# Turned products as three of 256 columns into one half bank, multiplied by the token row straight out of the bank

## The chip, the cores and the metric

The kernel runs on one NeuronCore of one Trainium2 chip. The metric is the time of one execution on the device in microseconds (us). TensorE (PE in the profile, with its loads of weights as PEld) multiplies, VectorE (DVE) and ScalarE (ACT) work on tiles in SBUF and in the eight banks of PSUM, SyncE (SP) issues the transfers, and GpSimd (POOL) a few small ones.

## The reference

Two transformer blocks on 256 tokens of width 2048, in float32. Cut to the lines that hold the large products:

```python
def first_block(x, ...):
    h = rmsnorm(x, attn_norm[l])
    qkv = jnp.einsum('bsd,de->bse', h, w_qkv[l])
    ...                                   # three attentions: y_a, y_b, y_c
    y = jnp.concatenate([y_a, y_b, y_c], axis=-1)
    x = x + jnp.einsum('bse,ed->bsd', y, w_o[l])
    h = rmsnorm(x, ffn_norm[l])
    g = causal_dwconv(jnp.einsum('bsd,df->bsf', h, w_gate[l]), conv_w[l], conv_b[l])
    u = jnp.einsum('bsd,df->bsf', h, w_up[l])
    x = x + jnp.einsum('bsf,fd->bsd', jax.nn.silu(g) * u, w_down[l])
    return rmsnorm(x, final_norm)
```

The second block projects `rmsnorm(x)` by `w_in` and two low rank paths, attends (latent attention, top-k attention, and a cross attention to 256 memory tokens), and ends with `x + square(relu(hm @ w_up)) @ w_down` and a last norm. Hidden widths are 5632 and 8192. The norm of a token is one number for each token, so it can be applied behind a product: it is the kernel's "token row".

## The kernel before

**Split numbers.** Every float32 operand of a large product is split into a high part, which TensorE's fp32r mode takes whole, and the rest: hi and lo. A product is then hi x hi + hi x lo + lo x hi. Activations stand as `xT[P, k, h, token]` (h = 0 hi, 1 lo; `mT` and `cT` likewise), turned so that the contracted dimension lies on the 128 partitions.

**Units.** The weights, 424 MB in all, pass once through the chip in 804 units of 1024 columns (512 KB). SP's queue brings a unit into one of four slots of `raw_w`, ScalarE writes `hi_w` (L840), VectorE writes `lo_w = raw_w - hi_w` (L1270), and PE uses both. The three engines each run the same list of units; `units(n)` in each engine's program takes the next n, with the splits running three units ahead of the products. Between calls of `units` stands the work of the attentions and norms, in an order written by hand.

**Groups.** Units form groups, each of which fills two banks, and the groups alternate between banks 0, 1 and 2, 3; PE starts a group when the group two before it has left its banks (`bank_out`). There are two kinds:
- straight groups (v, o, down, tail, and others; L465 to L467): a tile of 128 tokens of the activation is loaded as the weights of the array, and 512 columns of the streamed matrix pass through it, three products for each tile of 128 of the contracted dimension. The output has tokens on its partitions.
- turned groups (qk, gate, up1, q_nope, k_nope, kx, qx, up2; 104 groups): a 128 x 128 tile of the matrix is loaded, and the 256 tokens pass. The output has features on its partitions and is `out.T`. Each of a group's two tiles of 128 features has a bank of its own. These groups have up to 16 tiles of the contracted dimension and 4 units.

**A turned product before.** `w_hi` is loaded once and hi and lo of the activation pass together as 512 columns (L456): hi x hi goes to the first half of the bank, hi x lo to the second. `w_lo` then passes the 256 columns of hi, into the first half (L458). The two halves are added when the bank is emptied: ScalarE copies the second half out (L861, `part_out`), VectorE adds the first half to it (L1284, `sum_out`), and for the stages in `ROWED` VectorE multiplies the sum by the token row (L1289, `rowed`).

**What follows in the MLPs.** For a pair of gate tiles ScalarE makes the base of the convolution (L867), VectorE adds two taps (L1293, L1296), ScalarE takes tanh (L871) and VectorE forms silu (L1301). In up1 VectorE multiplies 0.5 x silu x up (L1307) and then by the token row (L1310), ScalarE writes the high part of the result (L877) and VectorE the low part (L1276). In up2 VectorE multiplies by the token row (L1317) and squares the positive part (L1320), then the same two parts follow (L883, L1276). L501 spreads a token row over the partitions; L482 and L512 are transposes.

## Time and profile before

| | |
|---|---|
| time, median of 3 runs | 2459.22 us (2454.11 to 2463.85) |
| the profiled execution | 2454.48 us, its span 2452.7 us |
| TensorE busy | 2403.1 us, 98% of the span |
| weight loads (PEld) | 2012.3 us |
| VectorE busy | 1562.8 us, 64% |
| ScalarE busy | 1248.1 us, 51% |
| DMA | 432.13 MB, mean 176 GB/s |
| mean granted clock | 0.996 |

The page gives busy time as the union of what an engine's instructions cover. Matmuls are pipelined: a product's record is longer than the distance from its start to the next one's, so the rate of TensorE is read from starts, in the timeline. A load of weights (PEld) lies beside the product before it.

### The profile page before, as it was taken

To read this page: it belongs to the slowest core of one execution; us is meant where nothing else is said; L and a number is where in the kernel's file an instruction comes from. 1 tells how busy PE (TensorE), PEld (TensorE's weight loads), DVE (VectorE), ACT (ScalarE), POOL (GpSimd) and SP (SyncE) were. 2 spreads that over 40 slices of the span, in tenths; PEclk is the share of its full clock that TensorE was granted. 3 is DMA by queue.
4 is the path that set the end of the run, shared out by engine and by line. 5 is a ranking of instruction groups with operands and counts; after the bars stand their busy time and mean duration, and the time that the engine had idled before them with its cause. 6 is when DMAs were issued, how large, how long until landed. Compare 5 with 4: busy or idle time off the path is not lost.

```text
span 2452.7 us, 32017 instructions
## 1 busy us (share of the span) xinstructions
PE 2403.1 (98%) x12314; PEld 2012.3 (82%) x12314; DVE 1562.8 (64%) x2437; ACT 1248.1 (51%) x1954; POOL 5.2 (0%) x12
## 2 busy tenths in 40 slices
PE   7999999999999999999999999999999999999998
PEld 6888877788888888888877877887888888888886
DVE  5687777777777557755667544664766556556454
ACT  5466566555555435544556445655544344344343
POOL 0000000000000000000000000000000000000000
PEclk9999999999999999999999999999999999999999
DMA  6544444455555565566564544554565665665664
GB/s 232 168 159 155 137 155 138 155 185 193 198 181 193 195 188 180 194 210 187 165 192 144 172 131 135 185 166 132 172 196 182 197 180 196 190 188 185 212 188 138
DMA packets 119063, 432.13 MB, mean 176 GB/s; under 512 B 13264, under 2 KB 13536, under 8 KB 118400
## 3 DMA queue, kind: packets, MB, share of 16 engines
q1 hardware_dynamic: 117936, 424.70, 54.3%
q0 software_dynamic: 976, 5.39, 0.6%
q8 instruction: 98, 1.61, 0.3%
q14 instruction: 53, 0.43, 0.1%
HBM read 427.93 MB, written 2.11 MB: 175 GB/s over the span
## 4 chain that ended last, share of the span: by engine, by line
PE 92%; DVE 4%; ACT 2%; issue 1%; DMA 1%; SPq 0%; ACTq 0%; DVEq 0%
PE bank L456 28%; PE bank L465 15%; PE bank L467 15%; PE bank L466 15%; PE bank L458 14%; DVE lo_w L1270 1%; PE bank L653 1%; DVE xT L1409 1%; ACT hi_w L840 1%; PE bank L482 1%; ACT xT L944 0%; DMA raw_w<-in_w_qk 0%; PE bank L637 0%; PE bank L526 0%; PE bank L607 0%
## 5 line engine op out<-in xcount | busy, mean ns | idle before, releaser
L1270 DVE TENSOR_TENSOR lo_w<-raw_w,hi_w 128x1024 fp32r<-128x1024 f32 x804 | 965.9, 1218 | 631.0 <-ACT hi_w L840 630.0
L840 ACT ACTIVATE hi_w<-raw_w 128x1024 fp32r<-128x1024 f32 x804 | 833.8, 1052 | 606.3 <-PE bank L467 417.8
L456 PE MATMUL bank<-xT,hi_w 128*128 128x512 f32 x3008 | 1054.0, 395 | 0.0
L458 PE MATMUL bank<-xT,lo_w 128*128 128x256 f32 x3008 | 839.5, 279 | 0.0
L456 PEld LDWEIGHTS bank<-xT,hi_w 128*128 128x128 f32 x3008 | 565.8, 188 | 128.8 <-issue 0.3
L458 PEld LDWEIGHTS bank<-xT,lo_w 128*128 128x128 f32 x3008 | 568.8, 189 | 0.5
L465 PE MATMUL bank<-hi_w,act_hi 128*128 128x512 f32 x864 | 341.4, 395 | 0.0
L467 PE MATMUL bank<-hi_w,act_lo 128*128 128x512 f32 x864 | 341.2, 395 | 0.0
L466 PE MATMUL bank<-lo_w,act_hi 128*128 128x512 f32 x864 | 341.2, 395 | 0.0
L465 PE MATMUL bank<-hi_w,xT 128*128 128x512 f32 (+1 forms) x736 | 294.2, 400 | 4.3 <-DVE xT L1409 3.5
L467 PE MATMUL bank<-hi_w,xT 128*128 128x512 f32 (+1 forms) x736 | 286.7, 389 | 0.0
L466 PE MATMUL bank<-lo_w,xT 128*128 128x512 f32 (+1 forms) x736 | 286.0, 389 | 0.0
L465 PEld LDWEIGHTS bank<-hi_w,act_hi 128*128 128x128 f32 x864 | 162.1, 188 | 39.5
L467 PEld LDWEIGHTS bank<-hi_w,act_lo 128*128 128x128 f32 x864 | 162.1, 188 | 39.5
L466 PEld LDWEIGHTS bank<-lo_w,act_hi 128*128 128x128 f32 x864 | 162.1, 188 | 38.9
L465 PEld LDWEIGHTS bank<-hi_w,xT 128*128 128x128 f32 x736 | 138.8, 189 | 32.0 <-issue 4.8
L467 PEld LDWEIGHTS bank<-hi_w,xT 128*128 128x128 f32 x736 | 138.6, 188 | 28.9
L466 PEld LDWEIGHTS bank<-lo_w,xT 128*128 128x128 f32 x736 | 138.9, 189 | 25.3
L1276 DVE TENSOR_TENSOR act_lo<-steps,act_hi 128x512 fp32r<-128x512 f32 x54 | 37.4, 693 | 39.3 <-ACT act_hi L883 23.6
L867 ACT ACTIVATE steps<-product,gains 128x256 f32<-128x256 f32 x44 | 26.5, 602 | 66.3 <-DVE product L1289 66.3
L861 ACT ACTIVATE product<-bank 128x256 f32<-128x256 f32 x88 | 33.4, 380 | 37.6 <-PE bank L458 37.6
L883 ACT ACTIVATE act_hi<-steps 128x512 fp32r<-128x512 f32 x32 | 20.3, 633 | 63.5 <-DVE steps L1320 63.5
(315 smaller groups left out, 1586.5 us busy)
## 6 DMA issues: line engine op xcount, KB each, us to landing
raw_w<-in_w_up SPq DMA_DIRECT2D x216, 512.0 KB, 4.2
raw_w<-in_w_down SPq DMA_DIRECT2D x216, 512.0 KB, 3.6
raw_w<-in_w_gate SPq DMA_DIRECT2D x88, 512.0 KB, 3.7
raw_w<-in_w_in SPq DMA_DIRECT2D x72, 512.0 KB, 3.8
raw_w<-in_w_qk SPq DMA_DIRECT2D x64, 512.0 KB, 3.6
raw_w<-in_w_v SPq DMA_DIRECT2D x32, 512.0 KB, 4.0
raw_w<-in_w_o SPq DMA_DIRECT2D x32, 512.0 KB, 3.5
raw_w<-in_w_out SPq DMA_DIRECT2D x32, 512.0 KB, 3.6
```

Source lines behind the costliest of these rows:

```text
L456: e.matmul(pair[c][:, :], w_hi[:, cols_k], both[:, kt].rearrange("p h t -> p (h t)"), start=(kt == 0), stop=False, skip_group_check=True)
L458: last = e.matmul(pair[c][:, 0:TOK], w_lo[:, cols_k], both[:, kt, 0, :], start=False, stop=(kt == g.kts - 1), skip_group_check=True)
L465: e.matmul(out, in_hi[:, at, rows], w_hi[:, cols_k], start=(kt == 0), stop=False)
L466: e.matmul(out, in_hi[:, at, rows], w_lo[:, cols_k], start=False, stop=False)
L467: last = e.matmul(out, in_lo[:, at, rows], w_hi[:, cols_k], start=False, stop=(kt == g.kts - 1))
L482: last = e.transpose(bank[:, k * TOK + t * P:k * TOK + (t + 1) * P], src[:, t, kt * P:(kt + 1) * P], const("ident"))
L653: last = e.matmul(banks[7][:, 0:wide], pT[:, k * P:(k + 1) * P], head_values(family, h, k), start=(k == 0), stop=(k == kts - 1))
L840: e.activation(hi_w[:, u % SPLIT_SLOTS, 0:unit_cols[u]], raw_w[:, u % RAW_SLOTS, 0:unit_cols[u]], ACT.Copy).then_inc(s["w_hi"], 1)
L861: e.activation(out, group_banks(n)[c][:, TOK:2 * TOK], ACT.Copy, scale=scale).then_inc(s["part_out"], 1)
L867: e.activation(conv1[:, pair % 2, c], out, ACT.Identity, bias=gain("convb", tile), scale=gain("conv2", tile)).then_inc(s["conv_base"], 1)
L1270: e.tensor_tensor(lo, raw_w[:, u % RAW_SLOTS, 0:unit_cols[u]], hi.bitcast(F32), ALU.subtract).then_inc(s["w_lo"], 1)
L1276: e.tensor_tensor(lo, prod[:, pair % 2], hi.bitcast(F32), ALU.subtract).then_inc(s[f"act_lo{tag}_done"], 1)
```

## The change

The two products for a tile of the contracted dimension become three, all of 256 columns and all into the first half of the bank: hi weights with hi, the same hi weights with lo, lo weights with hi. The second half of the bank is no longer used, so ScalarE's copy goes. VectorE empties the bank alone: with a scale, or with a scale and the token row in one instruction, straight out of the bank (`up2` is now among the stages in `ROWED`). In `up1` it multiplies 0.5 x silu by the bank directly; the token row of that stage is multiplied into silu in the gate group instead. Waits on `part_out` and `rowed` become waits on `w_used` and `sum_out`.

```diff
-ROWED = {"qk": "attn", "gate": "ffn", "kx": "mem", "qx": "cross"}
+ROWED = {"qk": "attn", "gate": "ffn", "kx": "mem", "qx": "cross", "up2": "mlp"}
...
                                 both = turned_in(g.stage)
                                 cols_k = slice(k * TURNED_COLS + c * P, k * TURNED_COLS + (c + 1) * P)
-                                e.matmul(pair[c][:, :], w_hi[:, cols_k], both[:, kt].rearrange("p h t -> p (h t)"),
-                                         start=(kt == 0), stop=False, skip_group_check=True)
-                                last = e.matmul(pair[c][:, 0:TOK], w_lo[:, cols_k], both[:, kt, 0, :],
-                                                start=False, stop=(kt == g.kts - 1), skip_group_check=True)
+                                out = pair[c][:, 0:TOK]
+                                e.matmul(out, w_hi[:, cols_k], both[:, kt, 0, :], start=(kt == 0), stop=False)
+                                e.matmul(out, w_hi[:, cols_k], both[:, kt, 1, :], start=False, stop=False)
+                                last = e.matmul(out, w_lo[:, cols_k], both[:, kt, 0, :],
+                                                start=False, stop=(kt == g.kts - 1))
...
             def diff_scores(i):
                 h, t = i // 2, i % 2
                 W, _ = token_tile(t)
-                e.wait_ge(s["rowed"], max(row_count["qk", h], row_count["qk", 8 + h]))
+                e.wait_ge(s["sum_out"], max(sum_count["qk", h], sum_count["qk", 8 + h]))
                 if i:
...
             def turned_group(g, n):
-                for c in range(2):
-                    tile, pair = 2 * g.part + c, g.part
-                    out, scale = turned_out(g.stage, tile)
-                    e.wait_ge(s["w_used"], 2 * g.last + 1 + c)
-                    if g.stage == "gate" and pair:
-                        e.wait_ge(s["prod1"], pair)
-                    if g.stage == "up1":
-                        e.wait_ge(s["conv_taps"], 4 * pair + 2 * (c + 1))
-                    if g.stage == "up2" and pair >= 2:
-                        e.wait_ge(s["act_lo2_done"], pair - 1)
-                    e.activation(out, group_banks(n)[c][:, TOK:2 * TOK], ACT.Copy,
-                                 scale=scale).then_inc(s["part_out"], 1)
-                    if g.stage == "gate":
-                        e.wait_ge(s["rowed"], row_count["gate", tile])
+                pair = g.part
+                if g.stage == "gate":
+                    for c in range(2):
+                        tile = 2 * pair + c
+                        e.wait_ge(s["sum_out"], sum_count["gate", tile])
                         if pair >= 2:
                             e.wait_ge(s["act_lo1_done"], pair - 1)
-                        e.activation(conv1[:, pair % 2, c], out, ACT.Identity, bias=gain("convb", tile),
+                        e.activation(conv1[:, pair % 2, c], product1[:, c, :], ACT.Identity, bias=gain("convb", tile),
                                      scale=gain("conv2", tile)).then_inc(s["conv_base"], 1)
-                if g.stage == "gate":
                     e.wait_ge(s["conv_taps"], 4 * pair + 4)
+                    if pair >= 2:
+                        e.wait_ge(s["act_lo1_done"], pair - 1)
                     e.activation(prod1[:, pair % 2], conv1[:, pair % 2], ACT.Tanh,
                                  scale=0.5).then_inc(s["gate_tanh"], 1)
                 elif g.stage == "up1":
                     if pair >= PHASE:
                         e.wait_ge(s["w_used"], 2 * (last_unit[f"down1_{pair // 8 - 2}"] + 1))
-                    e.wait_ge(s["prod1"], pair + 1)
+                    e.wait_ge(s["sum_out"], sum_count["up1", 2 * pair + 1])
                     e.activation(act_slot(pair, act_hi1, act_lo1)[0], prod1[:, pair % 2],
                                  ACT.Copy).then_inc(s["act_hi1_done"], 1)
...
             def turned_group(g, n):
+                pair, row = g.part, ROWED.get(g.stage)
+                if row:
+                    e.wait_ge(s["row_copied"], ROW[row] + 1)
+                if g.stage == "up1":
+                    pr = prod1[:, pair % 2]
+                    e.wait_ge(s["gate_rowed"], pair + 1)
                 for c in range(2):
-                    tile, pair = 2 * g.part + c, g.part
+                    tile, bank = 2 * pair + c, group_banks(n)[c][:, 0:TOK]
+                    e.wait_ge(s["w_used"], 2 * g.last + 1 + c)
+                    if g.stage == "up1":
+                        e.scalar_tensor_tensor(pr[:, c], pr[:, c], 0.5, bank, ALU.mult,
+                                               ALU.mult).then_inc(s["sum_out"], 1)
+                        continue
                     out, scale = turned_out(g.stage, tile)
-                    e.wait_ge(s["part_out"], sum_count[g.stage, tile])
-                    e.scalar_tensor_tensor(out, group_banks(n)[c][:, 0:TOK], scale, out,
-                                           ALU.mult, ALU.add).then_inc(s["sum_out"], 1)
-                    if g.stage in ROWED:
-                        e.wait_ge(s["sum_out"], sum_count[g.stage, tile])
-                        e.wait_ge(s["row_copied"], ROW[ROWED[g.stage]] + 1)
-                        e.tensor_tensor(out, out, token_rows[ROWED[g.stage]][:, :], ALU.mult).then_inc(s["rowed"], 1)
+                    if g.stage == "gate" and pair:
+                        e.wait_ge(s["conv_base"], 2 * pair)
+                        e.wait_ge(s["conv_taps"], 4 * pair)
+                    if g.stage == "up2" and pair >= 2:
+                        e.wait_ge(s["prod2"], pair - 1)
+                    if row:
+                        e.scalar_tensor_tensor(out, bank, scale, token_rows[row][:, :],
+                                               ALU.mult, ALU.mult).then_inc(s["sum_out"], 1)
+                    else:
+                        e.tensor_scalar(out, bank, scale, None, ALU.mult).then_inc(s["sum_out"], 1)
                     if g.stage == "gate":
                         after = conv1[:, pair % 2, c]
+                        e.wait_ge(s["sum_out"], sum_count["gate", tile])
                         e.wait_ge(s["conv_base"], 2 * pair + c + 1)
                         e.scalar_tensor_tensor(after[:, 1:TOK], out[:, 0:TOK - 1], gain("conv1", tile),
                                                after[:, 1:TOK], ALU.mult, ALU.add).then_inc(s["conv_taps"], 1)
...
                     e.wait_ge(s["gate_tanh"], pair + 1)
                     e.scalar_tensor_tensor(pr, pr, 1.0, conv1[:, pair % 2], ALU.add,
                                            ALU.mult).then_inc(s["gate_silu"], 1)
+                    e.wait_ge(s["gate_silu"], pair + 1)
+                    e.tensor_tensor(pr, pr, row_ffn[:, :].unsqueeze(1).to_broadcast([P, 2, TOK]),
+                                    ALU.mult).then_inc(s["gate_rowed"], 1)
                 elif g.stage == "up1":
-                    pr = prod1[:, pair % 2]
-                    e.wait_ge(s["gate_silu"], pair + 1)
                     e.wait_ge(s["sum_out"], sum_count["up1", 2 * pair + 1])
-                    e.scalar_tensor_tensor(pr, pr, 0.5, product1[:, :, :], ALU.mult,
-                                           ALU.mult).then_inc(s["prod_half"], 1)
-                    e.wait_ge(s["prod_half"], pair + 1)
-                    e.tensor_tensor(pr, pr, row_ffn[:, :].unsqueeze(1).to_broadcast([P, 2, TOK]),
-                                    ALU.mult).then_inc(s["prod1"], 1)
                     act_low(pair, 1, act_hi1, act_lo1, prod1)
                 elif g.stage == "up2":
                     cv = conv2[:, pair % 2]
                     e.wait_ge(s["sum_out"], sum_count["up2", 2 * pair + 1])
-                    e.wait_ge(s["row_copied"], ROW["mlp"] + 1)
-                    e.tensor_tensor(cv, cv, row_mlp[:, :].unsqueeze(1).to_broadcast([P, 2, TOK]),
-                                    ALU.mult).then_inc(s["up2_rowed"], 1)
-                    e.wait_ge(s["up2_rowed"], pair + 1)
+                    if pair >= 2:
+                        e.wait_ge(s["act_lo2_done"], pair - 1)
                     e.scalar_tensor_tensor(prod2[:, pair % 2], cv, 0.0, cv, ALU.max, ALU.mult).then_inc(s["prod2"], 1)
                     act_low(pair, 2, act_hi2, act_lo2, prod2)
```

On PE, at the start of the program, the first unit of qk (bank0 is the first tile's bank; L482 are the transposes ahead of it) stood before as:

```order
L482 MATMUL bank7<-consts,x 128x128 x4
L456 MATMUL bank0<-xT,hi_w 128x512
L458 MATMUL bank0<-xT,lo_w 128x256
L456 MATMUL bank0<-xT,hi_w 128x512
L458 MATMUL bank0<-xT,lo_w 128x256
```

and stands now as:

```order
L480 MATMUL bank7<-consts,x 128x128 x4
L454 MATMUL bank0<-xT,hi_w 128x256
L455 MATMUL bank0<-xT,hi_w 128x256
L456 MATMUL bank0<-xT,lo_w 128x256
L454 MATMUL bank0<-xT,hi_w 128x256
```

Two rows for a tile have become three, of 768 columns in all as before; each row stands for a load of weights and a product, so there is one load more too.

On VectorE, in the first MLP, one gate group (bank0, bank1) and the up1 group behind it (bank2, bank3), with the four splits of weights between them, stood before as:

```order
L1284 SCALAR_TENSOR_TENSOR product1<-bank0,product1 128x256
L1289 TENSOR_TENSOR product1<-product1,row1 128x256
L1293 SCALAR_TENSOR_TENSOR steps1<-product1,gains,steps1 128x255
L1296 SCALAR_TENSOR_TENSOR steps1<-product1,gains,steps1 128x254
...
L1301 SCALAR_TENSOR_TENSOR steps1<-steps1 128x512
L1270 TENSOR_TENSOR lo_w<-raw_w,hi_w 128x1024 x4
L1284 SCALAR_TENSOR_TENSOR product1<-bank2,product1 128x256
L1284 SCALAR_TENSOR_TENSOR product1<-bank3,product1 128x256
L1307 SCALAR_TENSOR_TENSOR steps1<-steps1,product1 128x512
L1310 TENSOR_TENSOR steps1<-steps1,row1 128x512
L1276 TENSOR_TENSOR act_lo1<-steps1,act_hi1 128x512
```

and stands now as:

```order
L1290 SCALAR_TENSOR_TENSOR product1<-bank0,row1 128x256
L1298 SCALAR_TENSOR_TENSOR steps1<-product1,gains,steps1 128x255
L1301 SCALAR_TENSOR_TENSOR steps1<-product1,gains,steps1 128x254
...
L1306 SCALAR_TENSOR_TENSOR steps1<-steps1 128x512
L1309 TENSOR_TENSOR steps1<-steps1,row1 128x512
L1260 TENSOR_TENSOR lo_w<-raw_w,hi_w 128x1024 x4
L1280 SCALAR_TENSOR_TENSOR steps1<-steps1,bank2 128x256
L1280 SCALAR_TENSOR_TENSOR steps1<-steps1,bank3 128x256
L1266 TENSOR_TENSOR act_lo1<-steps1,act_hi1 128x512
```

The row product behind each gate bank has gone into the instruction that empties it, and the 512 column row product has moved from behind the up1 banks to ahead of the four splits.

## Rows read from the trace of the kernel before

**Rows 1.** The page: span, busy shares, clock by slice, chain.
```profile
span 2452.7 us, 32017 instructions
...
PE 2403.1 (98%) x12314; PEld 2012.3 (82%) x12314; DVE 1562.8 (64%) x2437; ACT 1248.1 (51%) x1954; POOL 5.2 (0%) x12
...
PEclk9999999999999999999999999999999999999999
...
PE 92%; DVE 4%; ACT 2%; issue 1%; DMA 1%; SPq 0%; ACTq 0%; DVEq 0%
```

**Rows 2.** PE's groups by form: engine, operation, shapes, count | busy, mean ns.
```profile
L456 PE MATMUL bank<-xT,hi_w 128*128 128x512 f32 x3008 | 1054.0, 395 | 0.0
L458 PE MATMUL bank<-xT,lo_w 128*128 128x256 f32 x3008 | 839.5, 279 | 0.0
...
L456 PE MATMUL bank<-mT,hi_w 128*128 128x512 f32 x64 | 24.4, 419 | 0.0
...
L456 PE MATMUL bank<-cT,hi_w 128*128 128x512 f32 x48 | 17.8, 408 | 0.5 <-DVE q_nT L1284 0.5
```

**Rows 3.** PE's timeline, up2 stage, 70 pairs: start, length (us), instruction.
```profile
1799.88 0.39 PE L456 MATMUL bank<-xT,hi_w 128*128 128x512 f32 x1
1800.11 0.28 PE L458 MATMUL bank<-xT,lo_w 128*128 128x256 f32 x1
1800.23 0.39 PE L456 MATMUL bank<-xT,hi_w 128*128 128x512 f32 x1
...
1823.80 0.39 PE L456 MATMUL bank<-xT,hi_w 128*128 128x512 f32 x1
```

**Rows 4.** PE's timeline, a straight stage on xT, first and last of 32.
```profile
1242.75 0.39 PE L465 MATMUL bank<-hi_w,xT 128*128 128x512 f32 x1
...
1249.78 0.39 PE L466 MATMUL bank<-lo_w,xT 128*128 128x512 f32 x1
```

**Rows 5.** PE's timeline, last down stage, first and last of 66.
```profile
2299.77 0.40 PE L465 MATMUL bank<-hi_w,act_hi 128*128 128x512 f32 x1
...
2314.94 0.39 PE L467 MATMUL bank<-hi_w,act_lo 128*128 128x512 f32 x1
```

**Rows 6.** PE's timeline, tail stage, first and last of 40.
```profile
1206.78 0.34 PE L465 MATMUL bank<-hi_w,xT 128*128 128x400 f32 x1
...
1213.90 0.34 PE L465 MATMUL bank<-hi_w,xT 128*128 128x400 f32 x1
```

**Rows 7.** PE's timeline, kx stage, behind a wait of PE.
```profile
1623.56 0.63 PE L456 MATMUL bank<-mT,hi_w 128*128 128x512 f32 x1
1623.99 0.41 PE L458 MATMUL bank<-mT,lo_w 128*128 128x256 f32 x1
1624.20 0.63 PE L456 MATMUL bank<-mT,hi_w 128*128 128x512 f32 x1
```

**Rows 8.** Busy time by stretch, with the granted clock (PEclk).
```profile
core 0: us, PE busy (x) PEld busy (x) DVE busy (x) ACT busy (x) POOL busy (x), PEclk, DMA share, GB/s
1623.20:1625.20 2.00, 2.00 (x7) 1.69 (x7) 1.56 (x2) 0.00 (x0) 0.00 (x0) 0.50 0.73 244
```

**Rows 9.** PE's timeline, sixteen transposes on end and what follows.
```profile
1383.54 1.91 PE L512 MATMUL bank<-consts,staging 128*128 128x128 f32 x16
1385.20 0.48 PE L465 MATMUL bank<-hi_w,xT 128*128 128x512 f32 x1
```

**Rows 10.** ScalarE's groups by form, one of them.
```profile
L861 ACT ACTIVATE product<-bank 128x256 f32<-128x256 f32 x88 | 33.4, 380 | 37.6 <-PE bank L458 37.6
```

**Rows 11.** VectorE's groups by form.
```profile
L1317 DVE TENSOR_TENSOR steps<-steps,row 128x512 f32<-128x512 f32 x32 | 22.2, 693 | 1.1
...
L1289 DVE TENSOR_TENSOR product<-product,row 128x256 f32<-128x256 f32 x44 | 18.7, 425 | 1.5
L1307 DVE SCALAR_TENSOR_TENSOR steps<-steps,product 128x512 f32<-128x512 f32 x22 | 15.2, 693 | 2.7 <-DVE product L1284 0.5
L1310 DVE TENSOR_TENSOR steps<-steps,row 128x512 f32<-128x512 f32 x22 | 15.2, 692 | 0.7
```

**Rows 12.** PE's waits: line, for whom, total us, times, longest.
```profile
PE bank L501 <- DVE row_attn L1396: 4.6, 1, 4.6
PE bank L501 <- DVE row L1396: 4.4, 2, 2.3
...
PE bank L653 <- ACT a_pT L1043: 2.6, 6, 0.5
...
PE bank L775 <- ACT q_idxT L959: 0.8, 1, 0.8
...
PE bank L456 <- DVE q_nT L1284: 0.5, 1, 0.5
```

21 lines of the change are left out of this document (9 added, 12 removed).

## The prediction

> **What bounds the kernel now.** I read the page first: its busy shares, its row of the clock and its chain of work. TensorE is busy for 2403.1 of 2452.7 us, its granted clock is at the upper level (2.4 GHz) in every slice, and 92% of the chain that ended last is PE [rows 1]. VectorE and ScalarE have slack everywhere in the long stages. So a change that lightens them can give back at most the time in which PE stands still, 2452.7 - 2403.1 = 49.6 us, and a change to the products themselves counts in full.
>
> The second view groups PE's instructions by form. The turned stages make 3008 + 64 + 48 = 3120 pairs of a 512 column and a 256 column product [rows 2]; their durations there (395 and 279 ns) overlap, so they don't add up. What a product costs is the time from its start to the start of the next, and that stands in the timeline.
>
> Third, the timeline in four stretches without a wait. In the up2 stage the 512 column product starts at 1799.88 and the 69th after it at 1823.80 [rows 3]: 23.92 / 69 = 0.3467 us for a pair of 768 columns. In a straight stage that reads xT, 31 steps of 512 columns take 1249.78 - 1242.75 = 7.03 us, 226.8 ns each [rows 4]. In a down stage 65 such steps take 15.17 us, 233.4 ns each [rows 5]. In the tail stage 39 steps of 400 columns take 7.12 us, 182.6 ns each [rows 6].
>
> Last, the same pair while the granted clock is 0.50, its lower level (1.2 GHz), just after PE had waited: 1624.20 - 1623.56 = 0.64 us, that is 768 columns at exactly one per clock [rows 7, 8]. So columns alone would take 768 / 2.4 = 320.0 ns at the upper level, and each step there has something on top: 26.7 ns in a turned pair, 13.5 ns in the 512 column step on xT (213.3 for the columns), 20.1 ns in the down step, 15.9 ns in the 400 column step (166.7). This surplus is the number on which the case turns.
>
> **The change, part by part.**
> *Products.* For each of the 3120 pairs PE now runs three products of 256 columns, each with its own load of 128 x 128 weights. The columns are the same 768. What is added is one more product and one more load per pair: 3120 of each. The trace has no 256 column product of this type behind another, so I bound its step. From below: in the pair, the step that starts with the 256 column product lasts 0.11 to 0.12 us (1800.11 to 1800.23), and the other 0.23 [rows 3]. If the surplus goes with the columns (26.7 / 768 = 0.035 ns a column), three steps again take 346.7 ns and the edit costs nothing; if the shortest reading, 0.11, held for all three, 330 ns, it would give 16.7 x 3120 = 52 us back. The columns (320 ns) don't exclude that, but the two readings of a pair must sum to 346.7, so 0.11 is mostly the rounding of a row. From above: each product with its load pays the surplus of a down step, 20.1 ns, so that three take 3 x (106.7 + 20.1) = 380.4 ns, 33.7 more than now, x 3120 = 105 us.
>
> Between them I take a surplus per product of 13.35 ns. Two rows speak for it. The surplus of 400 columns (15.9 ns) isn't smaller than that of 512 on the same tile (13.5 ns), so it doesn't shrink with the columns [rows 4, 6]. And 26.7 ns for the two products of a pair is just twice 13.35, beside 13.5 for a lone 512 column product, where by columns the pair should have 1.5 times 13.5 = 20.2 [rows 3, 4]. That the 256 column step reads shorter than 120 ns (106.7 + 13.35) I explain by where the start is drawn: a load that is still being read can hold up the step behind it, and the two steps share 26.7 ns. With it three products take 320 + 40 = 360.0 ns, 13.3 more than now, and 3120 x 13.3 = **41.6 us** more on the path. This falls on PE, which has no cover.
>
> Can PE's loads or the feeding of instructions become the limit instead? Sixteen 128 column products with a load each pass in 1385.20 - 1383.54 = 1.66 us, 104 ns for load and product [rows 9]. That is below 115, so neither binds at 115 to 120 ns, at least in a run of 16; a longer run isn't in the trace.
>
> *ScalarE.* It no longer copies the second half bank: 208 instructions (two tiles for each of the 104 turned groups) at about 380 ns [rows 10], 79 us. All of that lies beside PE.
>
> *VectorE.* The product with the token row is folded into the one that empties the bank. Removed are 84 row products of 256 columns at 425 ns (32 qk, 44 gate, 4 kx, 4 qx), the 22 products L1307, which become part of emptying the up1 banks, and 32 of 512 columns in up2 at 693 ns: about 36 + 15 + 22 = 73 us, also beside PE [rows 11]. One is moved: the row product of the 22 pairs (692 ns) [rows 11] now stands in the gate group, ahead of the next four splits of weights. But VectorE starts that group without ScalarE's 380 ns copy, and without the 425 ns row product behind its last bank, so the splits come 0.69 - 0.38 - 0.425 = 0.1 us earlier than now. Emptying a bank now waits for PE directly, and nothing new is queued between.
>
> *Waits of PE.* Those that a lighter VectorE or ScalarE could shorten are small: 0.5 us before the first q_nope products, 2.6 us of values waiting for a copied a_pT, 0.8 us for a copied q_idxT, and others no longer than that. The largest, 4.6 and 4.4 us before L501, are for the token rows themselves, which come from sums over x and not from a turned group [rows 12]. The rows named here sum to 3.9 us and the smaller ones behind them perhaps double that, so I bound this at 0 and 10 us of the 49.6, and take 2, the lower part, since q_nT alone is emptied by a changed instruction.
>
> The sum against the profiled execution, 2454.5 us outside its span of 2452.7: 2454.5 + 41.6 - 2 = 2494 us. This execution was 4.7 us below the median of the three runs (2459.2), whose own spread is 10 us; against the median the sum is 2499. I predict 2497 us.
>
> **The rivals.**
> *A, the forecast, 50%:* a surplus per product and load, 2485 to 2515 us.
>
> *B, the surplus goes with the columns: no difference.* The direct reading speaks for it: the 256 column step lasts 0.11 to 0.12 us, half of the other's 0.23 [rows 3]. Then three take 346.7 to 350 ns, the sum changes by 0 to +10 us less 2, and the time is 2457 to 2467 us. This decides if a step stays under 118 ns (3 x 118 = 354, +7.3 x 3120 = 23 us, is halfway). Against it are the 400 column steps. 26%.
> The Trainium skill, page "TensorE: Matmul & The Clock Gate", section "Wait — 56ns, not 53.3ns?", has a fixed cost per matmul too, but of only about 2.5 ns at the upper clock. By it the 3120 further products would cost 3120 x 2.5 = 7.8 us, an estimate from the page, and the time would be inside this rival. The trace doesn't agree with that size for these products (13.5 to 20.1 ns on top of the columns), and at the lower clock it shows none, as the page says.
>
> *C, more than A:* stream and load collide more often in all-256 steps, with the down stage's 20.1 ns. Only the stationary tile differs between [rows 4] and [rows 5], so the surplus depends on what is read together, and reading hi and lo of xT as two streams may change it. Up to +105 us, 2562; halfway 2525. 16%.
>
> *D, faster by over 0.5%:* PE gets back its waits. All waits that the change can touch are about 10 us, less than the 12.3 us of that bound, so this needs steps below 115 ns as well, at 112 ns for instance (336 ns, -33 us, 2424). 8%.
>
> **How the numbers follow.** A and C are slower, B the same, D faster. About 0.5% (12 us) is what a measurement of this kernel can tell from no change. A lighter A (steps of 116 to 117 ns) still falls in the same: so 0.66 slower, 0.26 same, 0.08 faster. The range takes B's lower end less the runs' spread, 2452, and from C the lower half, 2528; D and the rest of C stay out, some 16%. A alone would be 2485 to 2515.
>
> **What the profile of the changed kernel would show.** Right: three rows of 256 columns per tile of 128, steps of 0.120 us, 0.360 for three in the up2 and gate stages; 3120 more PE and PEld instructions; PE's share still 98%; VectorE some 73 us and ScalarE some 79 us less busy; straight steps as before. Wrong by B: 0.345 to 0.350 for three. By C: 0.37 or more. Wrong altogether: PE idle at group starts, waiting for VectorE's L1290 or L1280, which would mean that emptying banks on one engine holds up PE; or PE's steps of uneven length with "issue" before them, which would mean that instructions are fed too slowly.

## The result and the profile after

| | before | after |
|---|---|---|
| time, median | 2459.54 us (2454.11 to 2463.85, 4 runs) | 2490.51 us (2488.05 to 2491.61, 4 runs) |
| ratio to before, 95% interval | | 1.0122 [1.0102, 1.0141] |
| span of the profiled execution | 2452.7 us | 2489.8 us |
| TensorE busy | 2403.1 us | 2440.4 us |
| VectorE busy | 1562.8 us | 1494.7 us |
| ScalarE busy | 1248.1 us | 1181.1 us |

The kernel became 1.2% slower, 31 us by the medians and 37 us by the two profiled spans. The profiled execution of before lay 5 us under its median, so 31 is the better figure for the kernels, and 37 the one that the two traces must account for.

The page of the changed kernel, with the lines that answer to [rows 1]: the span, the busy shares, the chain that ended last, and TensorE's three groups of turned products, which answer to the first two lines of [rows 2].

```profile
span 2489.8 us, 37911 instructions
...
PE 2440.4 (98%) x15434; PEld 2187.9 (88%) x15434; DVE 1494.7 (60%) x2299; ACT 1181.1 (47%) x1746; POOL 5.2 (0%) x12
...
PE 93%; DVE 3%; ACT 2%; issue 1%; DMA 0%; SPq 0%; ACTq 0%; DVEq 0%
...
L454 PE MATMUL bank<-xT,hi_w 128*128 128x256 f32 x3008 | 856.4, 285 | 0.9 <-DVE xT L1408 0.9
L455 PE MATMUL bank<-xT,hi_w 128*128 128x256 f32 x3008 | 852.9, 284 | 0.0
L456 PE MATMUL bank<-xT,lo_w 128*128 128x256 f32 x3008 | 852.7, 283 | 0.0
```

TensorE has 3120 products more (15434 against 12314). Its busy time grew by 37.3 us and the span by 37.1 us. The time in which it stands still is what it was, 49.4 us against 49.6. VectorE lost 68 us and ScalarE 67 us of work, and none of that shows in TensorE's idle time. The row of the granted clock reads 9 in every slice, as in [rows 1]. The whole difference of the two traces is therefore in the distance from one product's start to the next one's.

TensorE's timeline of the changed kernel in up2, the stretch that answers to [rows 3]:

```profile
1820.05 0.28 PE L454 MATMUL bank<-xT,hi_w 128*128 128x256 f32 x1
1820.17 0.28 PE L455 MATMUL bank<-xT,hi_w 128*128 128x256 f32 x1
1820.29 0.28 PE L456 MATMUL bank<-xT,lo_w 128*128 128x256 f32 x1
...
1833.85 0.28 PE L455 MATMUL bank<-xT,hi_w 128*128 128x256 f32 x1
```

From 1820.05 to 1833.85 are 115 steps: 13.80 / 115 = 0.1200 us, so 0.360 us for the three products, where the pair took 0.3467. No step is longer or shorter by more than the rounding. The down stage, which answers to [rows 5], has not changed: 43 steps from 2334.81 to 2344.84 give 0.2333 us.

```profile
2334.81 0.39 PE L463 MATMUL bank<-hi_w,act_hi 128*128 128x512 f32 x1
...
2344.84 0.40 PE L464 MATMUL bank<-lo_w,act_hi 128*128 128x512 f32 x1
```

Where the 37 us came in can be read from two places that both kernels pass: the first product of the first gate group, behind 512 turned steps of the contracted dimension, and the last turned product of all. In the timeline of the kernel before they stand at

```profile
456.94 0.39 PE L456 MATMUL bank<-xT,hi_w 128*128 128x512 f32 x1
...
2262.55 0.28 PE L458 MATMUL bank<-xT,lo_w 128*128 128x256 f32 x1
```

and in that of the changed kernel at

```profile
461.89 0.28 PE L454 MATMUL bank<-xT,hi_w 128*128 128x256 f32 x1
...
2299.69 0.28 PE L456 MATMUL bank<-xT,lo_w 128*128 128x256 f32 x1
```

At the first place the changed kernel is 4.95 us late, 9.7 ns for each of the 512 pairs. At the last one it is 37.14 us late. The 32.2 us between them lie on 2608 pairs: 2496 of them on xT, at 13.3 ns each 33.2 us, and 112 on mT and cT in the attention part, which cost nothing more (88 of them that no wait interrupts average 350.3 ns before and 351.3 after). About 1 us comes back at places between. Behind the last turned product nothing more is lost or won.

### The profile page after: what moved, and what is told of

It reads as the page before. It is cut to its first block, busy times and chain, and to the rows that moved or that the text cites. A ratio compares the mean times of both kernels' runs of the same rounds, so it can differ in the third digit from the quotient of the medians.

```text
span 2489.8 us, 37911 instructions
## 1 busy us (share of the span) xinstructions
PE 2440.4 (98%) x15434; PEld 2187.9 (88%) x15434; DVE 1494.7 (60%) x2299; ACT 1181.1 (47%) x1746; POOL 5.2 (0%) x12
## 4 chain that ended last, share of the span: by engine, by line
PE 93%; DVE 3%; ACT 2%; issue 1%; DMA 0%; SPq 0%; ACTq 0%; DVEq 0%
PE bank L463 15%; PE bank L454 15%; PE bank L465 15%; PE bank L464 15%; PE bank L455 15%; PE bank L456 15%; DVE lo_w L1260 1%; PE bank L651 1%; DVE xT L1408 1%; ACT hi_w L838 1%; PE bank L480 1%; DMA raw_w<-in_w_qk 0%; PE bank L635 0%; ACT xT L934 0%; PE bank L524 0%
## 5 line engine op out<-in xcount | busy, mean ns | idle before, releaser
L1260 DVE TENSOR_TENSOR lo_w<-raw_w,hi_w 128x1024 fp32r<-128x1024 f32 x804 | 972.2, 1219 | 741.1 <-ACT hi_w L838 740.1
L838 ACT ACTIVATE hi_w<-raw_w 128x1024 fp32r<-128x1024 f32 x804 | 840.5, 1054 | 755.6 <-PE bank L465 426.1
L454 PE MATMUL bank<-xT,hi_w 128*128 128x256 f32 x3008 | 856.4, 285 | 0.9 <-DVE xT L1408 0.9
L455 PE MATMUL bank<-xT,hi_w 128*128 128x256 f32 x3008 | 852.9, 284 | 0.0
L456 PE MATMUL bank<-xT,lo_w 128*128 128x256 f32 x3008 | 852.7, 283 | 0.0
L454 PEld LDWEIGHTS bank<-xT,hi_w 128*128 128x128 f32 x3008 | 579.4, 193 | 2.0 <-issue 1.4
L455 PEld LDWEIGHTS bank<-xT,hi_w 128*128 128x128 f32 x3008 | 579.3, 193 | 0.5
L456 PEld LDWEIGHTS bank<-xT,lo_w 128*128 128x128 f32 x3008 | 579.1, 193 | 0.0
```

The lines of the kernel that those rows point to most:

```text
L454: e.matmul(out, w_hi[:, cols_k], both[:, kt, 0, :], start=(kt == 0), stop=False)
L455: e.matmul(out, w_hi[:, cols_k], both[:, kt, 1, :], start=False, stop=False)
L456: last = e.matmul(out, w_lo[:, cols_k], both[:, kt, 0, :], start=False, stop=(kt == g.kts - 1))
L838: e.activation(hi_w[:, u % SPLIT_SLOTS, 0:unit_cols[u]], raw_w[:, u % RAW_SLOTS, 0:unit_cols[u]], ACT.Copy).then_inc(s["w_hi"], 1)
L1260: e.tensor_tensor(lo, raw_w[:, u % RAW_SLOTS, 0:unit_cols[u]], hi.bitcast(F32), ALU.subtract).then_inc(s["w_lo"], 1)
```

## The experiments

Two theories stood at the outset. PRODUCT says that every product with its load pays a fixed 13 to 20 ns on top of its columns, so that three products pay three times. COLUMNS says that the surplus belongs to the columns, and that the 31 us came in through something else: the accumulation into one half bank, or the emptying on VectorE. A third, PLACE, says that the surplus comes from where the two operands, the tile that is loaded and the tile that streams, lie in SBUF. A fourth, LOAD, says that a load of 128 columns itself takes 120 ns and is the limit. Times are medians, ratios are to the kernel before on the same chip. The experiments were run on three chips, and the changed kernel was not run again beside them; the kernel before had medians of 2457.75 to 2460.16 us there, so a difference in us to the changed kernel is good to some 2 or 3 us.

### Three products, into two half banks (x1_three_two_halves)

The kernel before, with only the products changed. The bank is emptied as before, ScalarE's copy included.

```diff
-    e.matmul(pair[c][:, :], w_hi[:, cols_k], both[:, kt].rearrange("p h t -> p (h t)"),
+    e.matmul(pair[c][:, 0:TOK], w_hi[:, cols_k], both[:, kt, 0, :],
              start=(kt == 0), stop=False, skip_group_check=True)
+    e.matmul(pair[c][:, TOK:2 * TOK], w_hi[:, cols_k], both[:, kt, 1, :],
+             start=False, stop=False, skip_group_check=True)
```

> The kernel before, with its products alone changed: three of 256 columns, but hi x lo still goes to the second half of the bank and is copied and added as before. If the whole loss comes from one more product with its load for each of the 3120 pairs, steps are 120 ns, three take 360, and the time is that of the changed kernel or up to 3 us more (before + 31 to + 37 us). If instead three products in a row into one and the same half bank are what costs (each waits for the one before it to be added up), steps are shorter here: 346.7 ns for three and the time of before (+ 0 to + 5 us).

Measured: 2492.62 us, 1.0137 [1.0109, 1.0166]. Its timeline in up2:

```profile
1819.94 0.28 PE L456 MATMUL bank<-xT,hi_w 128*128 128x256 f32 x1
...
1833.98 0.28 PE L456 MATMUL bank<-xT,hi_w 128*128 128x256 f32 x1
```

117 steps in 14.04 us, again 0.1200 us. The split of the product alone makes the whole loss. That all three results go to the same half bank, as they do in the changed kernel, costs nothing: with two halves the time is no shorter.

### The emptying alone (x2_emptying_alone)

The changed kernel with the two old products. The second half of the bank is filled but not read, so the term hi x lo is left out of the turned products' result.

```diff
-    out = pair[c][:, 0:TOK]
-    e.matmul(out, w_hi[:, cols_k], both[:, kt, 0, :], start=(kt == 0), stop=False)
-    e.matmul(out, w_hi[:, cols_k], both[:, kt, 1, :], start=False, stop=False)
-    last = e.matmul(out, w_lo[:, cols_k], both[:, kt, 0, :], ...)
+    e.matmul(pair[c][:, :], w_hi[:, cols_k], both[:, kt].rearrange("p h t -> p (h t)"), ...)
+    last = e.matmul(pair[c][:, 0:TOK], w_lo[:, cols_k], both[:, kt, 0, :], ...)
```

> The changed kernel with the old products (512 and 256 columns); the second half of the bank, hi x lo, is not read, so that term is left out of the turned products. Emptying and the rest are the changed kernel's. If VectorE and ScalarE are off the path, this is before - 0 to - 6 us. If their lighter load gives back real waits, it is before - 10 us or less. If emptying by VectorE alone holds up PE, it is slower than before.

Measured: 2456.15 us (10 runs), 0.9985 [0.9973, 0.9998], which is 3.7 us less than before (0.5 to 6.6). The changed emptying is no loss and is worth little, although it takes some 67 us of work off each of two engines. By the ratios x1 and x2 together account for the result: about +34 us from the products and about -4 us from the emptying, against +30.

One thing in its trace blurs the -4. No tile was moved and the products are those of the kernel before, yet the pairs of up2's first stretch (1734 to 1907 us) pass differently:

```profile
1800.16 0.40 PE L453 MATMUL bank<-xT,hi_w 128*128 128x512 f32 x1
...
1809.70 0.40 PE L453 MATMUL bank<-xT,hi_w 128*128 128x512 f32 x1
```

27 pairs take 9.54 us, 0.3533 each, where the kernel before has 0.3467 ([rows 3]). When up2 begins, this execution is 3.0 us ahead of the profiled one of before, and the 488 pairs of this stretch take that back (488 x 6.7 ns = 3.3 us). So even with the same products at the same places a stretch can run at one of two rates, and a few us of a kernel's time come from which it is.

### Another place in SBUF (x4_pad_192_0)

PLACE was tried by moving tiles without changing any instruction's work. Two unused tiles are allocated: 48 floats (192 bytes) ahead of xT, and 64 floats (256 bytes) behind `stats`, ahead of act_hi, act_lo, mT and cT.

```diff
         x = sbuf("x", [P, TT, D])
+        sbuf("pad_x", [P, 48])
         xT = sbuf("xT", [P, DK, 2, TOK], F32R)
 ...
         stats = sbuf("stats", [P, 192])
+        sbuf("pad_s", [P, 64])
```

In what follows the distance of a tile is its address in a partition minus that of `hi_w`, modulo 1024 bytes, from the order and the sizes of the kernel's allocations. In both kernels of the case it is 0 for xT, 576 for act_hi, act_lo and mT, and 192 for cT. Here it is 192 for xT, 0 for act and mT, and 640 for cT.

> The changed kernel with buffers moved in SBUF and nothing else: xT starts 192 bytes later against hi_w and lo_w (modulo 1024 bytes: 192 instead of 0), act_hi, act_lo and mT stand at 0 instead of 576, cT at 640 instead of 192. Theory PLACE (the surplus of a product depends on where the loaded and the streamed operand lie against each other): turned steps on xT fall from 120 to 113 ns, as they are in the k_nope stage (192 bytes), down steps from 233.4 to 226.8 ns, k_nope steps rise from 113; the time falls by 9024 x 7 = 63 us and 2592 x 6.7 = 17 us, to about 2410 us. Theory PRODUCT (a fixed surplus of 13.3 ns for each product): no step changes, 2490 us. Theory LOAD (a load of 128 x 128 itself takes 120 ns): no turned step changes.

Measured: 2438.24 us (2433.39 to 2440.15), 0.9913 [0.9888, 0.9938], 52 us less than the changed kernel and 21 us less than the one before. Its span is 2436.9 us. From its page:

```profile
PE 2387.9 (98%) x15434; PEld 2149.5 (88%) x15434; DVE 1491.9 (61%) x2299; ACT 1179.4 (48%) x1746; POOL 5.2 (0%) x12
```

The same 15434 products take 52.5 us less of TensorE (2440.4 before the move). Its timeline, first in a gate stretch, then in up2, then in down (lines 456 to 458 are here the turned products, 465 to 467 the straight ones):

```profile
599.90 0.28 PE L456 MATMUL bank<-xT,hi_w 128*128 128x256 f32 x1
...
613.84 0.28 PE L456 MATMUL bank<-xT,hi_w 128*128 128x256 f32 x1
...
1799.76 0.28 PE L456 MATMUL bank<-xT,hi_w 128*128 128x256 f32 x1
...
1813.90 0.28 PE L456 MATMUL bank<-xT,hi_w 128*128 128x256 f32 x1
...
2299.79 0.39 PE L466 MATMUL bank<-lo_w,act_hi 128*128 128x512 f32 x1
...
2309.99 0.39 PE L466 MATMUL bank<-lo_w,act_hi 128*128 128x512 f32 x1
```

In the gate stretch 123 steps take 13.94 us, 0.1133 each or 0.340 for three. In up2 120 steps take 14.14 us, 0.1178 each or 0.353 for three. In down 45 steps take 10.20 us, 0.2267 each, where they took 0.2333. One pattern holds for a whole stretch: 340 ns for the 998 sets of three between 468 and 807 us (but for one that meets a wait), 353 ns for all 383 between 895 and 1030 us and for the 996 from 1725 us on. The sum fits the span: 998 x 20.0 ns = 20.0 us, 1379 x 6.7 ns = 9.2 us, 2592 down steps x 6.7 ns = 17.3 us, and 6.3 us ahead of the first gate product (it starts 1.4 us earlier than before, where the changed kernel is 4.95 us later), together 52.8 us, where the spans differ by 52.9 (2489.8 - 2436.9). That it closes so well is in part luck: some 3 us that straight steps on xT lose (0.229 on average instead of 0.2267) are not in this sum, nor is about as much that other sets and waits give back.

The tiles that moved the other way confirm the direction. mT came from 576 to 0, and its turned products (stage kx), in the changed kernel and here:

```profile
1650.04 0.28 PE L454 MATMUL bank<-mT,hi_w 128*128 128x256 f32 x1
...
1660.99 0.28 PE L454 MATMUL bank<-mT,hi_w 128*128 128x256 f32 x1
```

```profile
1615.17 0.28 PE L456 MATMUL bank<-mT,hi_w 128*128 128x256 f32 x1
...
1625.97 0.28 PE L456 MATMUL bank<-mT,hi_w 128*128 128x256 f32 x1
```

93 steps in 10.95 us (0.1177) have become 90 steps in 10.80 us (0.1200). cT went from 192 to 640, and its sets of three from 353 or 340 ns to 360. That the loads themselves need 120 ns (LOAD) is excluded by the 113.3 ns of the gate stretch, with the same loads of 128 columns.

The time of about 2410 us that PLACE gave was not reached, because more than half of the long stretches (1379 of 2377 sets) run at 117.8 ns instead of 113.3. So the number of products was only half of the story. What a product pays depends on where its two operands lie.

### Down products in halves (x5_down_split)

The changed kernel, with every 512 column product of the down stages as two of 256 columns with the same tile loaded twice. The distance of this tile is 576.

```diff
+    if g.stage.startswith("down"):
+        for n_in, (tile, w) in enumerate(((in_hi, w_hi), (in_hi, w_lo), (in_lo, w_hi))):
+            for half in range(2):
+                ...
+                last = e.matmul(pair[c][:, part], tile[:, at, rows], w[:, at_w], ...)
+        continue
```

> The changed kernel with the down stages' 2592 products of 512 columns each split into two of 256 (the same tile loaded twice), into the two halves of the same bank. Theory PRODUCT with the surplus that these steps have now (20.1 ns): 2 x 126.8 = 253.5 instead of 233.4 ns, + 52 us; with 13.3 ns, 2 x 120 = 240, + 17 us. Theory LOAD: 2 x 120 = 240 ns, + 17 us. Theory COLUMNS (the surplus goes with the columns): 233.4 ns, + 0.

Measured: 2494.69 us, 1.0144 [1.0120, 1.0168]. Its timeline in down, where a row holds two products:

```profile
2329.76 0.40 PE L468 MATMUL bank<-hi_w,act_lo 128*128 128x256 f32 x2
...
2339.65 0.40 PE L468 MATMUL bank<-hi_w,act_lo 128*128 128x256 f32 x2
```

42 such rows take 9.89 us: 0.2355 us for two products of 256 columns and two loads, against 0.2333 for one of 512. The doubling of 2592 products cost some 4 us, where a fixed price of 20 ns for each would have cost 52. PRODUCT is refuted as a general rule, and so is LOAD, which gave 240 ns for two. At this place COLUMNS comes close, which it does not at xT's place.

### Four further places (y1_after_64, y2_after_320, z1_after_32, z3_after_96)

The changed kernel with pads of other sizes; act and mT stay at distance 0 in all four.

| | pad_x, pad_s (floats) | distance of xT |
|---|---|---|
| y1_after_64 | 16, 96 | 64 |
| y2_after_320 | 80, 32 | 320 |
| z1_after_32 | 8, 104 | 32 |
| z3_after_96 | 24, 88 | 96 |

> The changed kernel with xT 64 bytes beyond hi_w and lo_w (modulo 1024; as it was 0, in the run before 192) and act_hi, act_lo, mT at 0. Theory PLACE: the 256 column step on xT is neither 120 (distance 0) nor need it be the 115.7 of 192; anything from 109 to 120, to be read; down steps stay at 226.7. Theory PRODUCT had already to give way; what would bring it back is 120 here and at 320 too, with 192 alone an exception.

> As the run before, with xT 320 bytes beyond hi_w and lo_w. If the distance counts modulo 256 bytes, this reads as 64 does; if modulo 512 or more, differently. Down steps 226.7.

Measured, one run each: 2460.89 us and 2462.21 us. In both the long stretches run at 353 ns for three, and only short ones at 340; straight steps on xT are at 0.2333 instead of 0.2267, down steps at 0.2267. They are 30 and 28 us faster than the changed kernel, 17 of it from the down steps. The 340 ns of the gate stretch, which distance 192 showed, did not come.

> The changed kernel with xT 32 bytes beyond hi_w and lo_w, act and mT at 0, cT at 640. So far distances of 0 and 640 bytes gave 120 ns in every stretch, and 64, 192, 320, 576 gave either 113.3 or 117.8, one for a whole stretch: the distance seems to count modulo 128 bytes. 32 has not been seen. If only the parity of 64 byte pieces counts, 32 reads as 0: 360 ns for three and 2473 us (2490 - 17 for the down stages). If finer pieces count, it reads otherwise.

Measured: 2456.49 us, 0.9991 [0.9975, 1.0006]. In the gate stretch of its timeline

```profile
599.94 0.28 PE L456 MATMUL bank<-xT,hi_w 128*128 128x256 f32 x1
...
609.74 0.28 PE L456 MATMUL bank<-xT,hi_w 128*128 128x256 f32 x1
```

84 steps take 9.80 us, 0.1167 each or 0.350 for three, a value that no other place gave. That only whole 64 bytes count, so that 32 would behave as 0, is refuted.

> As the run before with 96 bytes. If only the parity of 64 byte pieces counts, it reads as 64: 340 or 353.3 ns for three in each stretch, and 2425 to 2462 us.

Measured: 2487.28 us, 1.0117 [1.0101, 1.0133], with steps of alternating length:

```profile
1800.01 0.28 PE L458 MATMUL bank<-xT,lo_w 128*128 128x256 f32 x1
1800.12 0.29 PE L456 MATMUL bank<-xT,hi_w 128*128 128x256 f32 x1
1800.25 0.28 PE L457 MATMUL bank<-xT,hi_w 128*128 128x256 f32 x1
1800.36 0.28 PE L458 MATMUL bank<-xT,lo_w 128*128 128x256 f32 x1
```

The three steps read 0.11, 0.13 and 0.11 us, and this goes on. The 340 or 353 ns that were expected, and a time of at most 2462 us, did not come. 84 steps from 1799.77 to 1809.85 us take 10.08 us, 0.1200 on average, as at distance 0. The 17 us that the down steps give here are eaten by the straight steps on xT: 2112 of them at 0.234 instead of 0.2267 cost 15 us.

### The kernel before at two other places (y3_before_0, y4_before_192)

y3 adds to the kernel before only `sbuf("pad_s", [P, 112])`: act and mT come to distance 0, xT stays at 0. y4 is the kernel before with the two pads of x4.

> The kernel BEFORE (512 and 256 columns, both halves of the bank) with act_hi, act_lo, mT moved from 576 to 0 bytes against hi_w, xT left at 0. Theory PLACE: down steps 233.4 to 226.7 ns, 2592 x 6.7 = 17 us less, turned pairs unchanged at 346.7: ratio 0.993. If the gain of the padded changed kernel came from something else that moved (VectorE, ScalarE), there is no such drop.

Measured: 2448.33 us (9 runs), 0.9959 [0.9945, 0.9972]. Its timeline in a gate stretch, and in a down stretch:

```profile
599.88 0.40 PE L457 MATMUL bank<-xT,hi_w 128*128 128x512 f32 x1
...
609.77 0.40 PE L457 MATMUL bank<-xT,hi_w 128*128 128x512 f32 x1
...
2299.67 0.39 PE L468 MATMUL bank<-hi_w,act_lo 128*128 128x512 f32 x1
...
2309.87 0.39 PE L468 MATMUL bank<-hi_w,act_lo 128*128 128x512 f32 x1
```

The down steps gained what was expected (10.20 us / 45 = 0.2267). The pairs in the gate stretch did not stay as they were: 28 pairs take 9.89 us, 0.3532 each against 0.3467, although neither xT nor `hi_w` was moved. In up2 the pairs run at 0.3467 until 1912 us and at 0.3533 later. In this profiled execution that gives back some 13 of the 17 us (1408 pairs in gate and up1 and about 510 in up2, at 6.7 ns), and its time, 2454.0 us, is the longest of its nine runs and hardly shorter than that of before (2454.5). By the ratio its runs are 10 us shorter than before's, so the patterns may differ between executions; the other runs have no trace to tell. The distance thus allows more than one pattern, as x2 showed too, and something else chooses between them when a stretch begins.

> The kernel BEFORE with the padding that brought the changed kernel to 2438 us (xT at 192, act_hi at 0). It tells whether three products or two are better in the same layout. By the columns alone 320 ns are common; the changed kernel has three products with 9.1 ns each on top (347.3). If two products pay the same 9.1 each, the pair takes 338 ns and this kernel is 3008 x 9 = 27 us faster than the changed one with padding, 2411 us. If the 512 column product pays more at 192 than at 0, as the straight steps on xT hint (229 instead of 228), pairs stay at 345 to 347 and the time is about 2440 us.

Measured: 2458.24 us (10 runs), 0.9991 [0.9979, 1.0002]. In up2 28 pairs from 1799.93 to 1809.83 us take 9.90 us, 0.3536 each, and it is the same in all long stretches. The down gain of 17 us is eaten by the pairs. Both times that the expectation named, 2411 and 2440 us, were missed: it took the surplus of a 512 column product to be that of a 256 column one, or the pair to stay at 347 ns. At this place three products beat two: x4 has the same pads and runs 20 us faster.

### Half of the weights loaded (x3_half_loads)

The changed kernel, whose up2 products load only 64 of the 128 columns of each weight tile. Half of up2's features are left out. The number of products, the streamed columns and their places are the same; each product writes 64 instead of 128 partitions of the bank.

```diff
+    wide = 64 if g.stage == "up2" else P
+    cols_k = slice(cols_k.start, cols_k.start + wide)
-    out = pair[c][:, 0:TOK]
+    out = pair[c][0:wide, 0:TOK]
```

> The changed kernel (xT at distance 0) where the up2 stage alone loads 64 instead of 128 weight columns for each product; half of its outputs are left out (old values stand there). Same products of 256 columns, 3072 of them. If the surplus of 13.3 ns comes from the reading of the weights beside the stream, half the reads should halve it: 113.3 ns a step, 20 us less. If a load of 128 columns takes 120 ns and is the limit, 64 columns take it away altogether: 109 ns or less, 34 us less. If it is fixed with each product: 120 ns, no change.

Measured, one run: 2472.0 us, span 2470.2. Its timeline in up2:

```profile
1799.76 0.28 PE L456 MATMUL bank<-xT,hi_w 128*64 128x256 f32 x1
...
1813.69 0.28 PE L456 MATMUL bank<-xT,hi_w 128*64 128x256 f32 x1
```

123 steps in 13.93 us are 0.1133 each with half of the load. In the gate stretch, which was not touched, 99 steps from 699.90 to 711.78 us stay at 0.1200. Of the surplus over the 106.7 ns that 256 columns take at 2.4 GHz, half is gone with half of the weights (13.3 to 6.6 ns). A price for one more instruction would have stayed. So the surplus comes with the halved part, beside the stream. Two reservations: 113.3 ns is also a value that x4 shows with full loads, and this run cannot tell a halved surplus from a jump to the next value that occurs (though no stretch at distance 0 in the changed kernel's trace runs at 113.3). And the edit halves what is written into the bank too, so it doesn't separate the weights that are read from the results that are written.

With x4, where only addresses in SBUF changed and the bank was left as it was, this suggests that the reading of the one operand holds up the other; it isn't shown directly. The Trainium skill says otherwise on the page "TensorE: Matmul & The Clock Gate", section "Step-by-step: what each phase is for": loading the next tile's weights "doesn't steal SBUF read bandwidth from the running matmul". The steps here are 6.7 ns shorter when half as much is loaded, so for these float32 products the measurement speaks against it, under the same reservations.

### Another order of the three (z4_order_192)

x4 with the order hi x hi, lo x hi, hi x lo, so that no two products behind each other load the same tile.

```diff
     e.matmul(out, w_hi[:, cols_k], both[:, kt, 0, :], start=(kt == 0), stop=False)
-    e.matmul(out, w_hi[:, cols_k], both[:, kt, 1, :], start=False, stop=False)
-    last = e.matmul(out, w_lo[:, cols_k], both[:, kt, 0, :],
+    e.matmul(out, w_lo[:, cols_k], both[:, kt, 0, :], start=False, stop=False)
+    last = e.matmul(out, w_hi[:, cols_k], both[:, kt, 1, :],
```

> The padded kernel of 2438 us (distance 192) with the three products in another order: hi weights x hi, lo weights x hi, hi weights x lo, so that no tile is loaded twice in a row. If the second load of the same tile costs something of its own, steps differ from 113.3 and 117.8. If the pattern alone counts, each stretch shows 340 or 353.3 ns for three again; which stretch gets which may change with the order, and with it the time, between 2420 and 2462 us.

Measured: 2439.29 us (8 runs), 0.9930 [0.9908, 0.9951], like x4, with 340 and 353 ns in the same long stretches as there. Loading one tile twice on end has no price of its own.

### The places together

| kernel | distance xT / act | three turned products, ns | straight step on xT | down step | us |
|---|---|---|---|---|---|
| after | 0 / 576 | 360 | 226.7 | 233.3 | 2490.5 |
| z1 | 32 / 0 | 350, some 353 | 233 | 226.7 | 2456.5 |
| y1 | 64 / 0 | 353, few 340 | 233 | 226.7 | 2460.9 |
| z3 | 96 / 0 | 360, uneven | 234 | 226.7 | 2487.3 |
| x4 | 192 / 0 | 340 (gate), 353 (up2) | 229 (mean of three) | 226.7 | 2438.2 |
| y2 | 320 / 0 | 353, few 340 | 233 | 226.7 | 2462.2 |

| kernel | distance xT / act | pair of 512 and 256, ns | down step | us |
|---|---|---|---|---|
| before | 0 / 576 | 346.7, short groups also 353 | 233.3 | 2459.5 |
| x2 | 0 / 576 | 346.7, 353 in up2's first stretch | 233.3 | 2456.2 |
| y3 | 0 / 0 | 353 (gate), 346.7 and 353 (up2) | 226.7 | 2448.3 |
| y4 | 192 / 0 | 353 | 226.7 | 2458.2 |

## Why the prediction was right, point by point

The prediction was 2497 us, in a range of 2452 to 2528, with slower at 0.66. Measured were 2490.5 us and slower. Forecast A held.

**The bound.** TensorE was at its limit and stayed there. What was taken off VectorE and ScalarE gave back about 4 us (x2: 0.5 to 6.6).

**The step of 120 ns.** The central step of the sum, 13.35 ns on top of the columns for each product with its load, gave 360.0 ns for three. The trace shows 360.0 in gate, up1 and up2. The argument for it was the 400 column row and the pair's two times 13.35. At xT's place it holds well enough: 13.3 ns on top of 256 columns and of 512 alike, 15.9 on top of 400. Its explanation of the shorter 256 column step in a pair (averaged over the 69 pairs of [rows 3] the starts are 0.230 and 0.117 us apart, where 0.2267 and 0.120 were assumed) was not tested, but the sum of the two is what counted. Rival B (by columns, under 118 ns a step) is refuted here. At act's place x5 comes out nearly as B says, and at distance 192 so do the turned products.

**What was luck.** The prediction took the 13.35 ns for a property of a product with its load. It is not one: x5 added 2592 products with loads for some 4 us instead of 35, and with xT 192 bytes further on the very products of the case take 113.3 or 117.8 ns. The step of 120 ns was right because both rows from which it was worked out, and the products to which it was applied, read the same tile at the same distance of 0. The prediction didn't know of the distance. In x4's layout the step from two products to three, with the emptying that goes with it, is worth 20 us less (y4 to x4) and not 31 us more.

**The term of 41.6 us was too large.** The same points in both timelines differ by 37.1 us. The 346.7 ns of a pair was read in up2, where it holds, and in gate too; but it was put to all 3120 pairs. The 512 pairs ahead of the first gate group stand in short runs between other work. There the added product cost 9.7 ns instead of 13.3: the threes that no wait interrupts average 359.6 ns as elsewhere, but the pairs averaged 349.9, since a part of the short groups already ran at 353 ns and not at 346.7. That is 1.9 us. The 112 pairs on mT and cT cost nothing, 1.5 us less, and about 1 us more comes back at places that the rows don't resolve. That leaves 37.1 us from end to end: 2454.5 + 37.1 = 2491.6, the profiled execution of the changed kernel, where the prediction had 2494. Between the medians there are only 31 us, so the 3 us that it added for the median of before, 2497, were not needed either. Why the medians lie closer than the traces is open. The runs of before spread over 10 us and those of the changed kernel over 4; that the pairs at distance 0 have two rates and the threes only one would fit this, but no other run has a trace to show it.

**The waits.** The -2 us cannot be told from nothing in the trace of the changed kernel (49.4 us idle against 49.6). By x2 it is 0.5 to 6.6 us, which the term of 2 lies within. The row product that was moved into the gate group made no wait of TensorE.

**ScalarE and VectorE.** 79 us and 73 us were expected, 67 and 68 came. These terms were off by 12 and 5 us on engines with some 900 us of slack or more. Part of ScalarE's difference is that its splits of weights cover 6.7 us more than before (840.5 against 833.8 us), and those of VectorE 6.3 us more (972.2 against 965.9), which is its whole difference.

**Rival C** was priced with the wrong sign. It said that stationary and stream collide depending on what is read together, and used this for a case above 360 ns. The dependence exists: the surplus changes with the place of the two operands, though by which mechanism is open. But distance 0 with its 120 ns is already the most expensive place found, with 96. In the kernel of the case it changed nothing, since the places stayed.

**The page's figure.** The estimate of 7.8 us from the 2.5 ns per matmul of the Trainium skill (page "TensorE: Matmul & The Clock Gate", section "Wait — 56ns, not 53.3ns?") was far too small for this layout: x1 shows 34 us for the same 3120 products.

## What to carry to other kernels

Where TensorE sets the end, read the distance of starts in every stage that the sum will use: a pair's 346.7 ns, read in the long stretches and put to all, made the term 4 us too large here. Joining two products into one with more streamed columns saved 13 ns a time at distance 0 and 2 ns at 576 (x5), and at 192 nothing or less (y4 against x4). So first try a pad of a few hundred bytes ahead of one operand: in this kernel that was worth 52 us with three products, more than the choice between two and three. The best version found is the changed kernel with x4's pads, 2438.2 us, 0.9913 of before; the same pads on the kernel before win nothing.

## What the runs showed that was not expected

Steps of these float32 products at a mean granted clock of 0.99 or more take a few fixed values, averaged over a set of three: 113.3, 116.7, 117.8 or 120.0 ns for 256 columns (106.7 for the columns alone), 226.7, 229.0, 233.3 or 234 for 512 (213.3 alone). Such a value holds over hundreds of products: x4's gate stretch shows 340 ns in all but one of its sets.

The distance in SBUF of the loaded and the streamed tile changes which values occur. For 256 columns those seen at 0 and at 640, whole multiples of 128 bytes, are 120.0; those at 64, 192, 320 and 576, the odd multiples of 64, are 113.3 or 117.8; at 32 there is 116.7 (and 117.8), at 96 an uneven 120.0. For 512 columns it is the other way round: 226.7 at 0, 229.0 at 192, and 233.3 or 234 at 32, 64, 96, 320 and 576. So placing xT better for the turned products worsens the straight ones on the same tile.

What chooses between the values allowed at one distance is open. In x4 it is 340 ns in one long stretch and 353 in the next, and so it is in z4; in y3 it changed in gate without a move of that stage's tiles, and in x2 in up2 without a move of any tile. If 340 could be had in all long stretches, the 1379 sets of three at 353 would give another 1379 x 13.3 ns = 18 us. The chip's part that makes loads and streams meet (a port, a bank of SBUF, a buffer ahead of the array) is not shown by any run: x3 shows only that half of the loaded columns, with half of the results, takes half of the surplus away, and the pads show that the address matters.
